# The retention gates as one half-size-products scheme over pairs of token tiles, with the steps reordered

## The chip, the cores and the metric

One NeuronCore of a Trainium2 chip. The metric is device time in microseconds of one execution. The whole model step is a single program with its instruction streams for TensorE (PE), VectorE (DVE), ScalarE (ACT), GpSimd (POOL) and SyncE (SP) written out by hand; the engines meet only at semaphores. All data are fp32.

## The reference

A two-layer diffusion trunk on 640 tokens: 512 latent and 128 prompt (context) tokens, five tiles of 128. Layer 0 mixes tokens by bidirectional retention with four heads, layer 1 by latent attention; each is followed by a mixture of experts. The change is in the retention layer:

```python
def step(s, xs):
    qc, kc, vc = xs
    att = einsum('bhnd,bhmd->bhnm', qc, kc) * intra
    o = einsum('bhnm,bhmv->bhnv', att, vc) + einsum('bhnd,bhdv->bhnv', qc * q_dec, s)
    s = s * c_dec + einsum('bhmd,bhmv->bhdv', kc * k_dec, vc)
    return s, o
...
q, k, v, g_f, g_b = split(h @ w_in)          # per head: q, k 256 wide, v, g_f, g_b 512 wide
o_f, s_f = retention_scan(q, k, v, ...)      # forward over chunks of 128 tokens
o_b, s_b = retention_scan(flip(q), ...)      # backward
y = silu(g_f) * head_layernorm(o_f, gn[0]) + silu(g_b) * head_layernorm(o_b, gn[1])
return y @ w_out, s_f, s_b
```

The prompt and the latent tokens are scanned apart: the prompt from a zero state, the latent tokens from a given one. The final prompt states are outputs.

## The kernel before

**Tiling.** `hT` holds the normalised input transposed, 8 slices of 128 features by 640 tokens (tiles 0 to 3 latent, tile 4, `PT`, prompt). Weights pass through five slots of 2 MB (`ring(0)` to `ring(4)`); slot 4 holds `XS`, sums of blocks of `hT`, in all heads. PSUM has eight banks of 128x512. The heads are head 0 (written out) and heads 1 to 3 (one loop body).

**A head.** First q and k (`products(h, 0, ...)`), then v (`products(h, 1, ...)`). Both already use the Strassen-Winograd scheme: for the 512 latent tokens, seven products of half-size blocks (`P1` to `P7`) in place of eight, with weight sums `T1` to `T4` made by DVE, a plain product `PR` for the prompt tile, and sums of the results by DVE (`u2`, `u3`, `C22`, `C21`, `C12`). In heads 1 to 3 the previous head's output projection (`out_proj`) stands between the two. Then the scores of five tiles (L1080), their masks by DVE (L1886, L1891), and ten steps.

**The steps.** `STEPS` lists the (tile, direction) pairs, latent ones first. In step i PE makes the output `o` in bank 5 (L1102; L1111 adds the part with the state, for latent tiles), updates the state where the step has one (L1119 into banks 6 and 7), transposes the next k (L1090), and makes the gate of this tile and direction: eight matmuls of 128x512 into one of banks 0 to 2 (L1127). Some steps also carry an eighth of the work on the modulation maps, a "slice" of `w_ada` (L891), and after four of them a panel transpose (L899). DVE: state update (L1912, or L1910 for the prompt), decayed k (L1897), statistics of `o` (L1919, L1921), normalisation (L1923, which frees bank 5), the gain (L1926), the gate (L1930, or L1932 and L1933 where the tile has its other direction already). POOL makes the reciprocal root (L776, L777) and the decayed q (L770). ACT applies silu to the gate bank (L1554).

**What sets the order.** Each engine's code, in order. PE's next step waits for L1923 of the last one, since there is one bank for `o`:

```python
if i:
    pe.wait_ge(S("o_free"), h * 10 + i)
```

**Borders.** After step 9 ACT writes the states out (L1564). In the next head it waits for `S_saved` (they have landed) and for the last step on DVE, issues three loads (L1542, L1544), and only then makes the copy `p1` (L1520) for which PE's `P2` of the q and k products waits:

```python
act.wait_ge(S("S_saved"), h * 32)
act.wait_ge(S("ln_done"), h * 10)
```

SP issues all weight loads through L524 in one written order, with a wait ahead of each for the last reader of its slot.

Of the kernel before, what the change touches and what calls it, by code (L numbers as in the profile page):

```python
# [39 lines left out]
STEPS = [(0, 0), (3, 1), (1, 0), (2, 1), (2, 0), (1, 1), (3, 0), (0, 1), (4, 0), (4, 1)]  # L40
STATE_STEPS = [0, 1, 2, 3, 4, 5, 8, 9]
NSS = len(STATE_STEPS)

SLICES_FIRST = {0: 0, 1: 1, 2: 2, 3: 3, 5: 4, 6: 5, 7: 6, 8: 7}
SLICES_LOOP = {1: 0, 3: 1, 5: 2, 7: 3}

SLOTS_FIRST = [0, 1, 0, 1, 0, 1, 0, 1]
SLOTS_LOOP = [0, 1, 0, 1]  # L50

PANELS_FIRST = {4: 1, 9: 2}
PANELS_LOOP = {8: None}
# [4 lines left out]


USES = 10  # L60
# [7 lines left out]

T_BANK = {0: (4, 6, 0, 2, 4), 2: (0, 0, 0, 0, 0)}
# [4 lines left out]
def use_base(h):  # L74

    return h * USES + PRE


def prod_no(h, f, name):

    return h * 16 + (f * 8 + PROD[name])


def add_no(h, f, name):

    return h * 18 + (4 + f * 9 + ADDS[name])


def copy_no(h, f, name):

    return h * 6 + (f * 3 + COPIES[name])
# [60 lines left out]
def build(nc, a, out):  # L152
    ctx = ExitStack()
    with ctx:
# [100 lines left out]
        sg = R["sg"].rearrange("p (b d) -> p b d", b=2)  # L255
        yy = R["y"].rearrange("p (t d) -> p t d", t=NT)
# [17 lines left out]
        def w_blocks(f, slot):  # L274
# [9 lines left out]
            return {"B11": b11, "B12": b12, "B21": b21, "B22": b22, "T1": b11, "T2": t2, "T3": b12, "T4": b21}  # L284

# [228 lines left out]
        def _(sp):  # L514
# [22 lines left out]
            for t in range(NT):  # L537
                src = a["x_prompt"][0] if t == PT else a["x_sample"][0, t * P:(t + 1) * P, :]
                sp.dma_start(x[:, t, :], src).then_inc(S(f"x_back{t}"), 16)

            def head_loads(h):
                first = isinstance(h, int)
                b = use_base(h)
                if not first:
                    sp.wait_ge(S("ada_done"), slices_done(h) - 1)
                for off in (0, RH * DK):
# [7 lines left out]
                for s, off in ((1, 2 * RH * DK), (2, 2 * RH * DK + RH * DV), (3, 2 * RH * DK + 2 * RH * DV)):  # L554
# [18 lines left out]
                else:  # L573
# [3 lines left out]
                    sp.wait_ge(S("op_done"), h * 10)  # L577
                    load_slice(1, h - 1, 1, SLOTS_LOOP[1])
                    sp.wait_ge(S("st_mm"), prod_no(h, 1, "P3"))
                    load_slice(1, h - 1, 0, SLOTS_LOOP[0])  # L580
                    for q in (2, 3):
                        sp.wait_ge(S("ada_done"), slices_done(h) + q - 1)
                        load_slice(1, h - 1, q, SLOTS_LOOP[q])
# [10 lines left out]
            sp.wait_ge(S("st_mm"), 16 * RH)  # L594
            load(4, ring(4).rearrange("p (j n) -> p j n", j=4), w_out[:, 12:16, :])

            def moe_loads(l):
# [6 lines left out]
                if l == 0:  # L604
                    sp.wait_ge(S("proj_done"), use_base(RH))
# [86 lines left out]
            for t in range(NT):  # L692
                sp.wait_ge(S("fin_ready"), t + 1)
                dst = out[0][0] if t == PT else out[1][0, t * P:(t + 1) * P, :]
# [7 lines left out]
        def _(pool):  # L702
# [55 lines left out]
            def head(h, per):  # L758
                def qdec_mul(u):
                    t, r = STEPS[u]  # L760
# [6 lines left out]
                    else:  # L767
                        pool.wait_ge(S("o_done"), h * 10 + u - 1)
# [5 lines left out]
                for i in range(10):  # L774
# [4 lines left out]
                    if i + 2 < 8:  # L779
                        qdec_mul(i + 2)  # L780
# [66 lines left out]
        def _(pe):  # L847
# [8 lines left out]
            def gate_bank_free(h, i):  # L856

                if i == 0:
                    pe.wait_ge(S("st_d"), add_no(h, 1, "C12"))
                elif i == 1:  # L860
                    pe.wait_ge(S("st_a"), copy_no(h, 1, "C11"))
                elif i >= 3:
                    pe.wait_ge(S("proj_evac"), use_base(h) + i - 2)

# [16 lines left out]
            def slice_of(h, panels_before, q, s):  # L881


                if q == 0:
                    pe.wait_ge(S("ada_act"), panels_before * 2)
                    pe.wait_ge(S("st_d"), add_no(h, 1, "C21"))
                pe.wait_ge(S(f"ring_full{s}"), full[s].next())
                for i in range(2):
                    k = 2 * q + i
                    for g in range(4):  # L890
                        mm = mmul(bank[3][32 * g:32 * g + 32, :], cond[:, 2 * k:2 * k + 32], ring2(s)[:, i, g * 512:g * 512 + 512],  # L891
# [74 lines left out]
            def out_proj(h, slot):  # L966
# [14 lines left out]
                for t in range(NT):  # L981
# [23 lines left out]
            def products(h, f, slot):  # L1005
# [17 lines left out]
                elif not first:  # L1023
                    pe.wait_ge(S("proj_evac"), use_base(h) - 2)
# [4 lines left out]
                elif not first:  # L1029
                    pe.wait_ge(S("ada_act"), h * 2 + 2)  # L1030
# [26 lines left out]

            def head(h):
# [3 lines left out]
                panels = PANELS_FIRST if first else PANELS_LOOP  # L1062
                b = use_base(h)
# [1234 lines left out]
```

## Time and profile before

| | us |
|---|---|
| median of 3 runs (lowest to highest) | 1860.96 (1854.48 to 1863.13) |
| the profiled execution's own time | 1861.93 |
| its span, first to last instruction | 1859.6 |
| PE busy | 1713.9 (92%) |
| DVE busy | 643.1 (35%) |
| mean granted TensorE clock, share of full | 0.964 |

An fp32 matmul stands in the trace as two PE instructions, so the eight matmuls of a gate are "x16". Matmul ends are modelled some 0.17 us late, so the start of one group to the start of the next is the better length. In a timeline, what stands in brackets is the idle time of the engine before the row and what ended it. Heads 0 to 3 end at about 240, 465, 685 and 905 us.

### The profile page before, as it was taken

What the parts mean: (1) busy time and instruction counts of PE and PEld (TensorE: products, weight loads), DVE (VectorE), ACT (ScalarE), POOL (GpSimd) and SP (SyncE); (2) the same over time, 40 slices, a digit from 0 to 9 for tenths busy, and PEclk for the clock granted to TensorE, in tenths of its full rate; (3) what the DMA queues carried; (4) which work ended last, traced back from release to release, by engine and by line L of the source; (5) the groups of instructions that cost most, each with busy time, mean ns of one, the idle gap of its engine ahead of it and who ended that gap; (6) DMA issues with size and microseconds to landing.
All of it is one profiled execution on the core that took longest, in us unless ns stands there. A gap on an engine that the chain in (4) does not pass through costs nothing.

```text
span 1859.6 us, 16869 instructions
## 1 busy us (share of the span) xinstructions
PE 1713.9 (92%) x6202; PEld 952.8 (51%) x6202; DVE 643.1 (35%) x1111; ACT 251.3 (14%) x538; POOL 180.8 (10%) x274
## 2 busy tenths in 40 slices
PE   4999999999999999999968999898999999689995
PEld 2864374644765456644444444354666664444442
DVE  2333323433233433333462332322333324423334
ACT  5000000000000000000121110321223221111111
POOL 1000000000001100010001222110000000012221
PEclk8999999999999999999987999999999999789998
DMA  9423452123412251112483999830000023749994
GB/s 339 160 91 136 147 212 90 46 91 136 147 45 90 74 183 70 67 68 90 148 293 125 342 341 349 251 119 0 23 22 5 7 81 124 238 128 342 345 344 139
DMA packets 159358, 281.21 MB, mean 151 GB/s; under 512 B 11428, under 2 KB 106424, under 8 KB 154184
## 3 DMA queue, kind: packets, MB, share of 16 engines
q1 hardware_dynamic: 144616, 236.39, 36.3%
q0 software_dynamic: 9248, 33.61, 6.9%
q10 hardware_dynamic: 5440, 10.49, 1.5%
q8 instruction: 34, 0.56, 0.1%
q14 instruction: 20, 0.16, 0.0%
HBM read 247.09 MB, written 33.37 MB: 151 GB/s over the span
## 4 chain that ended last, share of the span: by engine, by line
PE 78%; SPq 7%; DMA 7%; DVE 4%; issue 2%; ACT 1%; ACTq 0%; POOL 0%; DVEq 0%; POOLq 0%
PE banks L1127 15%; PE banks L1017 10%; PE banks L992 8%; PE banks L1189 7%; PE banks L1309 4%; PE banks L1408 4%; SPq L601 3%; PE banks L1206 3%; PE banks L1111 3%; PE banks L1119 3%; SPq L602 3%; PE banks L1102 2%; PE banks L891 2%; DMA wr<-in_moe_w_down 2%; PE banks L1341 2%
## 5 line engine op out<-in xcount | busy, mean ns | idle before, releaser
L1127 PE MATMUL banks<-wr 128*128 128x512 f32 x640 | 281.2, 592 | 0.0
L1189 PE MATMUL banks<-wr,arena 128*128 128x512 f32 x512 | 232.0, 607 | 9.8 <-DMA wr<-in_moe_w_down 6.5
L1127 PEld LDWEIGHTS banks<-wr 128*128 128x128 f32 x640 | 119.4, 190 | 139.7 <-issue 139.7
L1017 PE MATMUL banks<-wr 128*128 128x256 f32 x768 | 173.3, 385 | 4.1 <-ACT arena L1520 2.4
L1017 PEld LDWEIGHTS banks<-wr 128*128 128x128 f32 x768 | 147.8, 193 | 29.2 <-issue 4.5
L1189 PEld LDWEIGHTS banks<-wr,arena 128*128 128x128 f32 x512 | 96.9, 194 | 124.3 <-issue 123.5
L992 PE MATMUL banks<-wr,arena 128*128 128x512 f32 x320 | 142.9, 602 | 3.1 <-ACT arena L1514 3.1
L1206 PE MATMUL banks<-wr,arena 128*128 128x512 f32 x256 | 115.4, 593 | 0.9 <-ACT arena L1608 0.9
L992 PEld LDWEIGHTS banks<-wr,arena 128*128 128x128 f32 x320 | 60.4, 193 | 74.0 <-issue 72.0
L1554 ACT ACTIVATE arena<-banks 128x512 f32<-128x512 f32 x40 | 23.9, 597 | 520.4 <-PE banks L1127 520.4
L816 POOL DMA_INDIRECT acc_dram<-arena,put_ids x30 | 60.5, 2015 | 264.4 <-DVE arena L2065 264.4
L2050 DVE SCALAR_TENSOR_TENSOR arena<-banks,slot_w,arena 128x256 f32<-128x256 f32 x32 | 15.5, 484 | 183.2 <-ACT arena L1604 183.2
L1206 PEld LDWEIGHTS banks<-wr,arena 128*128 128x128 f32 x256 | 46.3, 190 | 48.3 <-issue 46.9
L1408 PE MATMUL banks<-wr,arena 128*128 128x512 f32 x160 | 70.3, 597 | 0.0
L2065 DVE TENSOR_TENSOR arena<-banks,arena 128x1024 f32<-128x1024 f32 x32 | 39.2, 1225 | 83.3 <-PE banks L1206 83.3
L1912 DVE SCALAR_TENSOR_TENSOR arena<-arena,cdec,banks 128x1024 f32<-128x1024 f32 x24 | 30.7, 1281 | 93.8 <-PE banks L1119 93.8
L1111 PE MATMUL banks<-arena 128*128 128x512 f32 x128 | 60.1, 592 | 0.0
L1119 PE MATMUL banks<-arena 128*128 128x512 f32 x128 | 60.1, 592 | 0.0
L770 POOL TENSOR_TENSOR arena<-arena 128x256 f32<-128x256 f32 x32 | 23.2, 730 | 376.5 <-DVE arena L1868 376.5
L1819 DVE TENSOR_TENSOR arena<-banks,arena 128x512 f32<-128x512 f32 x40 | 27.6, 691 | 84.6 <-PE banks L992 84.5
L1309 PE MATMUL banks<-arena 128*128 128x512 f32 (+1 forms) x192 | 54.0, 434 | 0.8 <-issue 0.8
L1359 PE MATMUL banks<-wr,arena 128*128 128x128 f32 x336 | 44.7, 277 | 8.0 <-DVE wr L2198 8.0
(269 smaller groups left out, 1968.1 us busy)
## 6 DMA issues: line engine op xcount, KB each, us to landing
wr<-in_w_ada SPq DMA_DIRECT2D x24, 2048.0 KB, 7.5
wr<-in_moe_w_gate SPq DMA_DIRECT2D x32, 1024.0 KB, 13.5
wr<-in_moe_w_up SPq DMA_DIRECT2D x32, 1024.0 KB, 16.2
wr<-in_moe_w_down SPq DMA_DIRECT2D x32, 1024.0 KB, 16.5
wr<-in_ret_w_in SPq DMA_DIRECT2D x12, 2048.0 KB, 10.7
wr<-in_ret_w_in SPq DMA_DIRECT2D x8, 1024.0 KB, 8.6
wr<-in_ret_w_out SPq DMA_DIRECT2D x4, 2048.0 KB, 7.6
arena<-mod_rows_dram SPq DMA_DIRECT2D x14, 512.0 KB, 6.8
```

What stands on the lines that cost most here:

```text
L601: sp.dma_start(gu[:, :, 1, :], w_u[l][e]).then_inc(S(f"w_full{b}"), 16)
L602: sp.dma_start(dn, w_d[l][e]).then_inc(S(f"w_full{b}"), 16)
L816: g.indirect_dma_start(out=acc[l], out_offset=bass.IndirectOffsetOnAxis(ap=put_ids[:, e:e + 1], axis=0), in_=ysb[:, b, :], in_offset=None, ...
L992: mm = mmul(bank[6 + hf][:], yT[:, t % 2, j, :], ring(slot)[:, j * D + hf * 512:j * D + hf * 512 + 512], start=(j == 0), stop=(j == 3))
L1017: mm = mmul(dst[:, r * 256:r * 256 + 256], lhs, rhs, start=(start and r == 0 and k == 0), stop=(k == 3), skip_group_check=True)
L1111: mm = mmul(bank[5][:], qd[:, i % 2, j, :], St[:, r, j, :], start=False, stop=(j == 1))
L1119: mm = mmul(bank[6 + j][:], kd[:, u % 2, tile_cols(j)], vv[:, t, :], start=True, stop=True)
L1127: mm = mmul(bank[i % 3][:], hT[:, k, tile_cols(t)], ring8(2 + r)[:, k, :], start=(k == 0), stop=(k == KT - 1))
L1189: mm = mmul(bank[2][:], xgT[:, e.par, k, :], expert_w(e.buf)[0][:, k].rearrange("p g f -> p (g f)"), start=(k == 0), stop=(k == KT - 1))
L1206: mm = mmul(bank[4 + 2 * e.par + hf][:], gactT[:, e.par, j, :], expert_w(e.buf)[1][:, j, hf * 512:hf * 512 + 512], start=(j == 0), stop=(j ...
L1309: mm = mmul(dst, lhs(k), rhs(k), start=(k == 0), stop=(k == nk - 1))
L1408: mm = mmul(bank[4 + hf][:], oTb[:, t % 2, k, :], w_o[:, k, hf * 512:hf * 512 + 512], start=(k == 0), stop=(k == KT - 1))
```

## The change

**Gates.** The ten gate products of a head are gone. The latent tiles are taken in pairs (0 and 1, the first half of the tokens; 2 and 3 the second), the forward and the backward gate weights (slots 2 and 3) as the two column blocks of one matrix, and the two halves of the features as its row blocks: the seven products of the scheme, each made for two tiles (`_0`, `_1`) with four matmuls of 128x512. The prompt tile keeps two plain products (`PR_0`, `PR_1`) of eight. That is 56 + 16 = 72 matmuls a head where there were 80. The weight sums are made in place by DVE, `T1`, `T2` ahead of step 0, `T3` after step 0, `T4` after step 1, each of 128x2048; ten result sums of 128x512 follow from step 1 on.

**Order.** `P1_0`, `P1_1`, `PR_0`, `PR_1` stand ahead of step 0, the others after steps 0 to 7, none after steps 8 and 9. The prompt's steps are first and have no state work there; step i (from 2) now does state i - 2. Tiles are held in the order 0, 1, 3, 2 (`ORDER`). In head 0 the first four slices go to bank 7 around steps 0 and 1.

```diff
-STEPS = [(0, 0), (3, 1), (1, 0), (2, 1), (2, 0), (1, 1), (3, 0), (0, 1), (4, 0), (4, 1)]
-STATE_STEPS = [0, 1, 2, 3, 4, 5, 8, 9]
-SLICES_LOOP = {1: 0, 3: 1, 5: 2, 7: 3}
+STEPS = [(4, 0), (4, 1), (0, 0), (2, 1), (1, 0), (3, 1), (3, 0), (1, 1), (2, 0), (0, 1)]
+STATES = [(0, 0), (2, 1), (1, 0), (3, 1), (3, 0), (1, 1), (4, 0), (4, 1)]
+SLICES_LOOP = {4: 0, 5: 1, 6: 2, 8: 3}
+SLICES_FIRST = {4: 4, 5: 5, 6: 6, 7: 7}
+SLOTS_LOOP = [1, 0, 1, 1]
+GBANK = {"P1_0": 1, "P2_0": 1, "P5_0": 1, "P3_0": 1, "P1_1": 0, "P2_1": 0, "P5_1": 0, "P3_1": 0, "PR_0": 3, "PR_1": 2,
+         "P6_0": 2, "P7_0": 2, "P6_1": 2, "P7_1": 2, "P4_1": 3, "P4_0": 3}
+AFTER_STEP = {0: ("P2_0", "P2_1"), 1: ("P6_0", "P7_0"), 2: ("P5_0", "P6_1"), 3: ("P7_1", "P5_1"), 4: ("P4_1",),
+              5: ("P3_1",), 6: ("P4_0",), 7: ("P3_0",)}
@@ SyncE, loads of a head
                     if s == 2 and not first:
-                        sp.wait_ge(S("proj_done"), b - 1)
+                        sp.wait_ge(S("st_mm"), gate_prod(h, "P4_0") - 32)
                     if s == 3 and not first:
-                        sp.wait_ge(S("proj_done"), b)
+                        sp.wait_ge(S("st_mm"), gate_prod(h, "P3_0") - 32)
@@ TensorE
+            def gate_product(h, name):
+                ...
+                elif p == "P7":
+                    pe.wait_ge(S("st_d"), gate_add(h, "u2_" + tile))
+                elif name == "P6_1":
+                    pe.wait_ge(S("st_d"), gate_add(h, "u3_0"))
+                ...
+                    cols = tile_cols(int(tile))
+                    for k in range(4):
+                        mm = mmul(dst, X[X_OF[p]][:, k, cols], W[p][:, k, :], start=(k == 0 and p not in ("P2", "P7", "P3")),
+                                  stop=(k == 3), skip_group_check=True)
+                mm.then_inc(S("st_mm"), 1)
                 ...
+                gate_product(h, "P1_0")
+                gate_product(h, "P1_1")
                 ...
+                pe.wait_ge(S("attm"), h * 4 + 4)
                 k_T(0)
+                gate_product(h, "PR_0")
+                gate_product(h, "PR_1")
                 ...
-                    for k in range(KT):
-                        mm = mmul(bank[i % 3][:], hT[:, k, tile_cols(t)], ring8(2 + r)[:, k, :],
-                                  start=(k == 0), stop=(k == KT - 1))
-                    mm.then_inc(S("proj_done"), 1)
+                    for name in AFTER_STEP.get(i, ()):
+                        gate_product(h, name)
@@ VectorE
+                sums = {1: ("u2_0", "T4", "u3_0"), 2: ("C22_0", "u2_1"), 3: ("u3_1", "C22_1"), 4: ("C21_1",), 5: ("C12_1",),
+                        6: ("C21_0",), 7: ("C12_0",)}
                 k_decay(0)
+                weight_sum("T1")
+                weight_sum("T2")
                 ...
+                    if i == 0:
+                        weight_sum("T3")
+                    for name in sums.get(i, ()):
+                        if name == "T4":
+                            weight_sum(name)
+                        else:
+                            gate_sum(name)
```

On DVE the statistics and the normalisation were behind the state update in a step; now the statistics are ahead of it. ACT copies `P1_0`, `P1_1`, and applies silu to four results in PSUM and to six in SBUF.

**The order of the instructions.** DVE in head 0, from the second weight sum to the sums after step 1. First what is there now (L1986 is `T2`, L1988 `T3`, L1992 `T4`, L2002 `u2_0` and `u3_0`, L2041 frees bank 5):

```order
L1986 TENSOR_TENSOR arena<-wr 128x2048 [waits st_d]
L2025 BN_STATS st<-banks 128x6 [waits o_done,gn_in,S_in]
L2027 BN_AGGR mv<-st 128x2 [waits dve_step]
L2041 TENSOR_SCALAR arena<-banks,mv,rv 128x512 [waits head_rstd]
L2044 TENSOR_TENSOR arena<-arena 128x512 [waits o_free]
L2049 TENSOR_TENSOR arena<-arena 128x512 [waits st_a,dve_step]
L1988 TENSOR_TENSOR wr<-wr 128x2048 [waits ln_done]
L2025 BN_STATS st<-banks 128x6 [waits o_done]
...
L2052 TENSOR_TENSOR arena<-arena 128x512 [waits dve_step]
L2002 TENSOR_TENSOR arena<-banks,arena 128x512 [waits st_a,st_mm,ln_done]
L1992 TENSOR_TENSOR wr<-arena,wr 128x2048 [waits st_mm,st_d]
L2002 TENSOR_TENSOR arena<-banks,arena 128x512 [waits st_a,st_mm]
```

Before, the first steps of DVE in head 0:

```order
L1897 TENSOR_SCALAR arena<-banks,kdec 128x256 [waits kt_done]
L1912 SCALAR_TENSOR_TENSOR arena<-arena,cdec,banks 128x1024 [waits S_done,gn_in,S_in]
L1897 TENSOR_SCALAR arena<-banks,kdec 128x256 [waits kt_done]
L1919 BN_STATS st<-banks 128x6 [waits o_done]
L1921 BN_AGGR mv<-st 128x2 [waits dve_step]
L1923 TENSOR_SCALAR arena<-banks,mv,rv 128x512 [waits head_rstd]
L1926 TENSOR_TENSOR arena<-arena 128x512 [waits o_free]
L1930 TENSOR_TENSOR arena<-arena 128x512 [waits proj_evac,dve_step]
```

Three weight sums and the whole of step 1 now stand ahead of the first `u2_0`; the state work has left these two steps.

PE in head 0, step 1 (L1170, `o`) with `P6_0`, `P7_0` and the panel transpose behind it, as it is now:

```order
L1170 MATMUL banks<-arena 128x512 [waits o_free]
L1116 MATMUL banks<-arena,wr 128x512 [waits st_d,st_a]
L1116 MATMUL banks<-arena,wr 128x512 x3
L1116 MATMUL banks<-wr 128x512 [waits st_d]
L1116 MATMUL banks<-wr 128x512 x3
L925 MATMUL banks<-ident,stage 128x128 [waits ada_act]
L925 MATMUL banks<-ident,stage 128x128 x3
```

Step 1 of PE before:

```order
L1102 MATMUL banks<-arena 128x512 [waits o_free]
L1111 MATMUL banks<-arena 128x512 [waits S_in,qd_ready]
L1111 MATMUL banks<-arena 128x512
L1119 MATMUL banks<-arena 128x512 [waits S_upd,kd_ready]
L1119 MATMUL banks<-arena 128x512
L1090 MATMUL banks<-ident,arena 128x128 [waits kd_ready]
L1090 MATMUL banks<-ident,arena 128x128
L1127 MATMUL banks<-wr 128x512 [waits ring_full3,st_a]
L1127 MATMUL banks<-wr 128x512 x7
```

The gate's eight matmuls waited for nothing that DVE makes within the steps; the second half of the eight that stand there now (`P7_0`, the second `st_d`) waits for a sum of the first.

SP keeps its order of loads. What changed is when the waits are met: slots 2 and 3 of the next head are free after steps 6 and 7, but their loads stand behind that of `w_out`, which waits for the last slice, now after step 8.

## Rows read from the trace of the kernel before

**Rows 1.** The page's first part: busy time of each engine.
```profile
PE 1713.9 (92%) x6202; PEld 952.8 (51%) x6202; DVE 643.1 (35%) x1111; ACT 251.3 (14%) x538; POOL 180.8 (10%) x274
```

**Rows 2.** Busy us of each engine in one 50 us stretch.
```profile
350.00:400.00 50.00, 50.00 (x146) 21.26 (x146) 19.11 (x29) 2.39 (x4) 5.74 (x12) 1.00 0.17 65
```

**Rows 3.** Waits (engine, line, releaser: us in total, times, longest).
```profile
PE banks L1090 <- DVE arena L1891: 5.8, 4, 1.5
...
PE banks L1017 <- ACT arena L1520: 2.4, 2, 1.4
```

**Rows 4.** Timeline of PE, one step of head 3 (start us, us, instructions).
```profile
801.50 1.02 PE L1102 MATMUL banks<-arena 128*128 128x512 f32 x2
...
804.08 1.88 PE L1119 MATMUL banks<-arena 128*128 128x512 f32 x4
805.80 0.38 PE L1090 MATMUL banks<-ident,arena 128*128 128x128 f32 x2
806.01 7.03 PE L1127 MATMUL banks<-wr 128*128 128x512 f32 x16
812.98 1.92 PE L891 MATMUL banks<-wr,cond 128*32 128x512 f32 x16
814.83 1.12 PE L1102 MATMUL banks<-arena 128*128 128x512 f32 x2
```

**Rows 5.** Timeline of DVE, steps 7 and 8 of head 3.
```profile
876.77 0.70 DVE L1919 BATCH_NORM_STATS2 st<-banks 128x6 f32<-128x512 f32 x1 [0.45 <-PE banks L1111]
...
878.74 0.81 DVE L1923 TENSOR_SCALAR arena<-banks,mv,rv 128x512 f32<-128x512 f32 x1 [0.93 <-POOL rv L777]
879.59 0.69 DVE L1926 TENSOR_TENSOR arena<-arena 128x512 f32<-128x512 f32 x1
...
888.34 1.23 DVE L1910 COPY arena<-banks 128x1024 f32<-128x1024 f32 x1 [2.57 <-PE banks L1119]
889.48 0.48 DVE L1897 TENSOR_SCALAR arena<-banks,kdec 128x256 f32<-128x256 f32 x1
889.88 0.69 DVE L1919 BATCH_NORM_STATS2 st<-banks 128x6 f32<-128x512 f32 x1
```

**Rows 6.** Timeline of DVE, two sums of 128x1024.
```profile
695.86 1.23 DVE L1850 TENSOR_TENSOR wr<-wr 128x1024 f32<-128x1024 f32 x1 [8.47 <-PE banks L1035]
697.12 1.23 DVE L1852 TENSOR_TENSOR arena<-wr 128x1024 f32<-128x1024 f32 x1
```

**Rows 7.** Timeline of PE after its longest waits near the heads.
```profile
242.20 0.28 PE L1138 MATMUL banks<-ident,mod 128*96 128x128 f32 x1 [2.34 <-DVE mod L1753]
242.52 5.40 PE L1017 MATMUL banks<-wr 128*128 128x256 f32 x16
...
907.42 1.18 PE L978 MATMUL banks<-ident,arena 128*128 128x128 f32 x8 [2.22 <-DVE arena L1933]
910.35 9.49 PE L992 MATMUL banks<-wr,arena 128*128 128x512 f32 x16 [1.75 <-ACT arena L1514]
```

**Rows 8.** Timeline of PE, the border between heads 2 and 3.
```profile
685.06 3.62 PE L1017 MATMUL banks<-wr 128*128 128x256 f32 x16
...
696.85 3.72 PE L1017 MATMUL banks<-wr 128*128 128x256 f32 x16 [1.02 <-ACT arena L1520]
```

**Rows 9.** Timeline of ACT, the same border.
```profile
685.49 0.96 ACTq L1564 DMA_DIRECT2D out<-arena  x2
694.59 0.41 ACTq L1542 DMA_DIRECT2D arena<-in_state_ret_fwd  x1
...
696.20 0.60 ACT L1520 ACTIVATE arena<-banks 128x512 f32<-128x512 f32 x1 [10.26 <-PE banks L1035]
```

**Rows 10.** ACT queue, DMAs issued at 46 us (KB each, us to landing).
```profile
arena<-in_state_ret_fwd ACTq DMA_DIRECT2D x1, 512.0 KB, 7.2
arena<-in_state_ret_bwd ACTq DMA_DIRECT2D x1, 512.0 KB, 9.5
```

**Rows 11.** DMAs issued on SP's queue from 33 to 44 us.
```profile
wr<-in_ret_w_in SPq DMA_DIRECT2D x3, 2048.0 KB, 20.2
```

More of the change, by code:

```diff
@@ L66 @@
 COPIES = {"p1": 1, "PR": 2, "C11": 3}
+GPROD = ("P1_0", "P1_1", "PR_0", "PR_1", "P2_0", "P2_1", "P6_0", "P7_0", "P5_0", "P6_1", "P7_1", "P5_1",
+         "P4_1", "P3_1", "P4_0", "P3_0")
+GADDS = ("T1", "T2", "T3", "u2_0", "T4", "u3_0", "C22_0", "u2_1", "u3_1", "C22_1", "C21_1", "C12_1", "C21_0", "C12_0")
+GCOPIES = ("p1_0", "p1_1", "PR_0", "PR_1", "C11_0", "C11_1", "C22_0", "C22_1", "C21_1", "C12_1", "C21_0", "C12_0")
+GBANK = {"P1_0": 1, "P2_0": 1, "P5_0": 1, "P3_0": 1, "P1_1": 0, "P2_1": 0, "P5_1": 0, "P3_1": 0, "PR_0": 3, "PR_1": 2,
+         "P6_0": 2, "P7_0": 2, "P6_1": 2, "P7_1": 2, "P4_1": 3, "P4_0": 3}
+AFTER_STEP = {0: ("P2_0", "P2_1"), 1: ("P6_0", "P7_0"), 2: ("P5_0", "P6_1"), 3: ("P7_1", "P5_1"), 4: ("P4_1",),
+              5: ("P3_1",), 6: ("P4_0",), 7: ("P3_0",)}
+GATE_OF = {(4, 0): "PR_0", (4, 1): "PR_1", (0, 0): "C11_0", (2, 1): "C22_0", (1, 0): "C11_1", (3, 1): "C22_1",
+           (3, 0): "C21_1", (1, 1): "C12_1", (2, 0): "C21_0", (0, 1): "C12_0"}
 T_BANK = {0: (4, 6, 0, 2, 4), 2: (0, 0, 0, 0, 0)}
@@ L255, in build @@
         sg = R["sg"].rearrange("p (b d) -> p b d", b=2)
+        late = R["yT"].rearrange("p (b d) -> p b d", b=2)
         yy = R["y"].rearrange("p (t d) -> p t d", t=NT)
@@ L1056, in products @@
                 product("P3", False)
+            def gate_product(h, name):
+                W = gate_w(isinstance(h, int))
+                p, tile = name.split("_")
+                if name == "P1_0":
+                    pe.wait_ge(S("ring_full2"), full[2].next())
+                    pe.wait_ge(S("st_a"), copy_no(h, 1, "C11"))
+                elif name == "P1_1":
+                    pe.wait_ge(S("st_d"), add_no(h, 1, "C12"))
+                elif name == "PR_1":
+                    pe.wait_ge(S("ring_full3"), full[3].next())
+                elif p == "P2":
+                    pe.wait_ge(S("st_a"), gate_copy(h, "p1_" + tile))
+                elif name == "P6_0":
+                    pe.wait_ge(S("st_a"), gate_copy(h, "PR_1"))
+                    pe.wait_ge(S("st_d"), gate_add(h, "T2"))
+                elif p == "P7":
+                    pe.wait_ge(S("st_d"), gate_add(h, "u2_" + tile))
+                elif name == "P6_1":
+                    pe.wait_ge(S("st_d"), gate_add(h, "u3_0"))
+                elif p == "P5":
+                    pe.wait_ge(S("st_a"), gate_copy(h, "C11_" + tile))
+                elif name == "P4_1":
+                    pe.wait_ge(S("st_a"), gate_copy(h, "PR_0"))
+                    pe.wait_ge(S("st_d"), gate_add(h, "T4"))
+                elif p == "P3":
+                    pe.wait_ge(S("st_d"), gate_add(h, "C22_" + tile))
+                elif name == "P4_0":
+                    pe.wait_ge(S("st_d"), gate_add(h, "C21_1"))
+                dst = bank[GBANK[name]]
+                if p == "PR":
+                    for k in range(KT):
+                        mm = mmul(dst, hT[:, k, TS:T], ring8(2 + int(tile))[:, k, :], start=(k == 0), stop=(k == KT - 1))
+                else:
[4 more added lines that the diff above has]
+                mm.then_inc(S("st_mm"), 1)
             def head(h):
```

250 lines of the change are left out of this document (147 added, 103 removed).

## The prediction

> **What bounds the kernel now.** I read the busy times first: PE is at 92% of the span, DVE at 35% [rows 1]. The averages hide stages, so next the windows: within the steps of a head PE is busy for all of 50 us at full clock, DVE for 19.1, ACT for 2.4 [rows 2]. The steps are bound by PE; a matmul taken out there is worth its length as long as DVE keeps up. Then the list of waits, for what PE stands still for in the heads: 1.45 us each for the masks (5.8 in four), and 1.0 and 1.4 at two borders between heads, for a copy by ACT [rows 3]. Last the timelines of PE and DVE, since the change turns independent products into a chain through DVE.
>
> **The unit prices.** A step of PE, by starts [rows 4]: `o` of a latent tile 2.58, the state 1.72, the k transposes 0.21, a gate of eight matmuls 6.97 with its hand-over, a slice 1.85. The gate and the slice together are 8.82, which I split as 6.9 and 1.9; four matmuls are 3.45, one 0.86. On DVE [rows 5]: statistics to normalisation 1.97 (POOL's root is in it), normalisation 0.85, each 128x512 operation after it about 0.72; a state update 1.14 to its follower, the decayed k 0.40. PE to DVE takes 0.2 to 0.3, DVE to PE about 0.1. A weight sum is 128x2048, a size the trace lacks. 128x1024 takes 1.23 [rows 6] and 128x512 takes 0.69 [rows 5]; the same slope gives 2.3 us. Bounds: 1.23 (as if size cost nothing) and 2.46 (twice). I take 2.3.
>
> **Removed, every head.** Eight matmuls net: -6.9. The mask wait: `P1_0` and `P1_1` now lie under it, -1.45 [rows 3].
>
> **Added, heads 1 to 3: the chain at `P7_0`.** Zero is the end of `PR_1` on PE. DVE can start `T1` at 0.2, so `T2` ends at 4.8. PE meanwhile makes `o` of step 0 (0.9) and `P2_0`, `P2_1` (7.7). DVE: statistics of step 0 at 4.8, normalisation 6.75 to 7.55, so bank 5 is free just as PE wants it; gain and gate to 9.0; `T3` to 11.3. PE: step 1 to 8.6, `P6_0` to 12.0. Only at 11.3 does DVE turn to step 1: 1.97 + 0.85 + three times 0.72 brings 16.3, `u2_0` 17.0. `P7_0` adds into the bank that `u2_0` reads, so PE stands from 12.0 to 17.0: **+5.0 us**. Behind it on PE's queue stand step 2 and all later ones. After this nothing in DVE's chain is late: `P6_1` finds `u3_0` done (step 2 lies between), `T4` is wanted only after step 4, and from step 4 on a step of PE is 2.58 + 1.72 + 0.21 + 3.45 = 8.0 or more, against 7.2 of DVE (1.98 to the state's end on PE, 1.14, 0.40, 0.85, three of 0.72, one sum of 0.7).
>
> **The end of the steps.** Bank 5 is free again 1.98 + 1.14 + 0.40 + 0.85 = 4.4 us after `o` ends. Step 8 has no gate product any more: 1.72 + 0.21 + slice 1.9 = 3.8 of work, so PE waits 0.6 before step 9. In head 0 step 8 has no slice either: 1.93 of work, 2.5 of wait. Net, without the clock: heads 1 to 3 -6.9 - 1.45 + 5.0 + 0.6 = **-2.8 each**.
>
> **The clock.** PE ran at full clock after waits of 1.0 and 1.4 (16 half-size instructions in 3.72 [rows 8]), but after a wait of 2.34 the same 16 took 5.40, and after 2.22 and 1.75 close together 16 of 128x512 took 9.49 where 7.0 is usual [rows 4, 7]: 1.8 and 2.5 us lost at half clock, 1.2 in place of 2.4 GHz. A wait of 5.0 is longer than all of these. I charge 1.8, bounds 0 and 2.5, to each new wait above 2.2: heads 1 to 3 come to -1.0 each, **-3.0**.
>
> **Head 0.** Two slices lie in the first part and give DVE time on PE's side: step 1's `o` ends at 12.5, `P6_0` at 16.0, `u2_0` at 18.4, a wait of 2.4. With 2.5 before step 9 and 1.8 of clock for both: -6.9 - 1.4 + 2.4 + 2.5 + 3.6 = +0.2. At its end PE's transpose of the modulation rows waits for DVE (2.34 now [rows 7]). DVE's last step was under a gate product; now it starts with PE's last matmuls and ends 1.98 + 1.14 + 0.85 + three of 0.72 = 6.1 after `o`, 4.0 after PE's last work at 2.15, and three small operations follow: 4.7 in place of 2.3, **+2.4**.
>
> **The borders before heads 2 and 3.** PE stops at 685.06, wants `p1` at 685.06 + 10.8, and gets it 1.0 late [rows 8]. ACT had issued the states at 685.49, their landing let it go on at 694.59, 1.6 us of issues and a copy of 0.6 follow [rows 9]. Now the last state is updated 3.1 us after step 9's `o`, so the issue comes 1.1 after PE's end, not 0.43: +0.7. And more is in flight: `w_out` and slots 2 and 3, 6 MB, are released together about 5 us before PE's end, where one load of 2 MB was. What does that do to 1 MB on ACT's queue? At 46 us two loads of that size landed in 7.2 and 9.5 us [rows 10] while SP's queue held 2 MB loads that took 20.2 each [rows 11]: ACT's queue is not made to wait for SP's. So 9.1 becomes 9.5 to 10: +0.2 to +0.8. Waits of about 2.2 and 2.6, **+1.2 each**, and in half of them the clock falls, +0.9 each: +4.2 for both. Before head 1 PE arrives later than ACT and nothing changes. After head 3 the projection's transposes wait 4.0 for DVE, not 2.2, and its first matmuls come at 6.2 after PE's end, not 5.3: +0.9 [rows 7].
>
> The Trainium skill ("DMA: Bandwidth & Descriptors", Queues, rings and completion order) says two things that pull apart: each DMA engine takes turns between its queues packet by packet, which would give the states their half; but a completion semaphore is a strongly ordered write that lands only after all earlier writes of that engine, also those of other queues. Rows 10 and 11 bear out the first; by the second alone the borders would come out as in the second rival.
>
> **The sum.** -3.0 + 0.2 + 2.4 + 4.2 + 0.9 = **+4.7** on the profiled execution's 1861.9 (span 1859.6): 1866.6. It is 1.0 above the median of the runs, so I predict 1865.5. The case's own bounds: no clock lost at all and +0.6 a border gives -8.4 - 3.4 + 2.4 + 1.2 + 0.9 = -7.3 (1853.5 as a median); 2.5 of clock at every wait and +1.5 a border gives +12.0 (1873).
>
> **The rivals.**
> *The gain is paid out.* If DVE's chain never reached PE, only the removed work would count: 4 x 6.9 + 5.8 = -33, some 1828. For it: DVE is at 35%. Against: the timeline has PE and DVE in lock-step through one bank, and the average says nothing of steps 0 and 1, where DVE has 17 us of work for PE's 12. 5%.
> *The weight sums are cheap.* At 1.23 each (the lower bound) `u2_0` comes 3.2 us earlier, the wait is 1.8 and the clock stays up: 3 x (3.2 + 1.8) = 15 less, 1850.5. The two rows of different size speak against it. 8%.
> *The states wait for all weights* (the slow side). If a landing is told only when all that was issued before has drained, then from the 9.1 us that 3 MB (1 MB of states, 2 MB of slot 3) take at this border now [rows 9], the 5.7 MB left then take some 17: PE waits 9 at the two borders instead of 1.0 and 1.4, +9.8 each with the clock, +19.6 in place of +4.2: 1881. It decides as soon as the landing takes over 11. Rows 10 and 11 are against it. 12%.
> *The change doesn't save what it says:* the program counts 72 for 80, so no.
>
> **Chances.** The forecast 75%, its own range 1853.5 to 1873; above 1870.3 lies a tenth of the whole. A measurement of this kernel can't tell less than 0.5% (9.3 us) from no change. Faster by more: 5 + 8 and a little of the forecast's low end, 16%. Slower by more: 12 + 10, 22%. The rest, 62%, within. Range 1851 to 1875.
>
> **What would show it.** After: PE L1116 waiting about 5 us, three times, for DVE L2002, once 2.4 in head 0, with a slow window behind; L1170 waiting 0.6 in heads 1 to 3 and 2.5 in head 0 for L2041; PE L1153 waiting for no mask; DVE at 128x2048 2.3 us; the `p1` copy's wait at two borders 2 to 3 us; L1206 waiting 4.7. PE's matmul count falls by 64 instructions. I am wrong in the size if the wait for L2002 is below 3 us, or if full clock follows it; wrong in kind if the heads get shorter by over 5 us, or if PE waits for a DMA (a slice) in a step.

## The result and the profile after

The changed kernel takes 1867.41 us (median of 9 runs) where the kernel before took 1861.54 beside it: ratio 1.0031 [1.0019, 1.0044]. It is slower by about 6 us, which is within 0.5%. One of the nine runs took 2084.41 at a granted clock of 0.826, and the ratio leaves it out. The profiled execution took 1864.86 (span 1862.5, mean granted clock 0.960), against 1861.93, 1859.6 and 0.964.

The page's first part, to be held against [rows 1]: 20 us less of PE, 63 more of DVE.

```profile
PE 1693.8 (91%) x6138; PEld 944.5 (51%) x6138; DVE 706.0 (38%) x1167; ACT 257.4 (14%) x546; POOL 180.8 (10%) x274
```

So PE does 20 us less and the span is 2.9 longer: 23 us went into standing still. The list of PE's waits in the four heads (us in total, times, longest) says where; it answers to [rows 3].

```profile
PE banks L1116 <- DVE arena L2002: 17.4, 4, 5.0
PE banks L1043 <- ACT arena L1588: 6.6, 2, 3.5
PE banks L1206 <- DVE mod L1832: 4.3, 1, 4.3
PE banks L1004 <- DVE arena L2052: 3.9, 1, 3.9
PE banks L1170 <- DVE arena L2041: 3.3, 4, 2.2
PE banks L1043 <- DVE arena L1931: 2.7, 1, 2.7
```

The mask waits are gone. In their place stand the chain at `P7_0` (first row), the borders before heads 2 and 3 (second), the ends of heads 0 and 3 (third, fourth), bank 5 before step 9 (fifth), and one that the prediction didn't have: `P6` of head 1's q and k, which waits for a weight sum (sixth).

Head 1's steps 0 to 2 on PE (start, duration, group, in brackets the idle time before it):

```profile
370.12 1.02 PE L1170 MATMUL banks<-arena 128*128 128x512 f32 x2
370.98 7.03 PE L1116 MATMUL banks<-wr 128*128 128x512 f32 x16
377.85 1.02 PE L1170 MATMUL banks<-arena 128*128 128x512 f32 x2
378.71 3.60 PE L1116 MATMUL banks<-wr 128*128 128x512 f32 x8
387.33 6.46 PE L1116 MATMUL banks<-wr 128*128 128x512 f32 x8 [5.03 <-DVE arena L2002]
```

DVE in the same 17 us, from `T1` (L1983) to `u2_0` (the last row):

```profile
370.32 2.29 DVE L1983 TENSOR_TENSOR wr<-wr 128x2048 f32<-128x2048 f32 x1 [13.14 <-PE banks L1112]
372.65 2.29 DVE L1986 TENSOR_TENSOR wr<-wr 128x2048 f32<-128x2048 f32 x1
374.86 0.69 DVE L2025 BATCH_NORM_STATS2 st<-banks 128x6 f32<-128x512 f32 x1
...
379.21 2.29 DVE L1988 TENSOR_TENSOR wr<-wr 128x2048 f32<-128x2048 f32 x1
381.42 0.69 DVE L2025 BATCH_NORM_STATS2 st<-banks 128x6 f32<-128x512 f32 x1
...
385.77 0.69 DVE L2052 TENSOR_TENSOR arena<-arena 128x512 f32<-128x512 f32 x1
386.58 0.69 DVE L2002 TENSOR_TENSOR arena<-banks,arena 128x512 f32<-128x512 f32 x1
```

From 370.32 on DVE stands still only for POOL's root (0.94 us each time) and for 0.16 us behind each of the statistics. `o` of step 1 ends on PE at about 378.8, but `T3` holds DVE until 381.4, and the whole of step 1's normalisation stands ahead of `u2_0`. PE waits 5.03 us for a sum of 0.69. The window answers to [rows 2]: PE busy 44.97 us where it was 50, DVE 21.12, and the granted clock 0.93 where it was 1.00 (busy us of PE, PEld, DVE, ACT, POOL, then the clock).

```profile
350.00:400.00 50.00, 44.97 (x102) 19.68 (x101) 21.12 (x26) 3.58 (x6) 2.92 (x7) 0.93 0.00 0
```

The border before head 2, PE and then ACT. At the next one, that of [rows 8] and [rows 9], the wait was 3.08 and the landing took 10.6.

```profile
466.04 3.62 PE L1043 MATMUL banks<-wr 128*128 128x256 f32 x16
469.49 7.31 PE L1059 MATMUL banks<-wr 128*128 128x128 f32 x64
480.29 5.41 PE L1043 MATMUL banks<-wr 128*128 128x256 f32 x16 [3.49 <-ACT arena L1588]
```

```profile
467.06 0.94 ACTq L1643 DMA_DIRECT2D out<-arena  x2
478.05 0.41 ACTq L1618 DMA_DIRECT2D arena<-in_state_ret_fwd  x1
...
479.64 0.60 ACT L1588 ACTIVATE arena<-banks 128x512 f32<-128x512 f32 x1 [13.08 <-issue]
```

The states go out 1.0 us after PE's last work, as forecast, and ACT goes on 11.0 us later. "Landing" below is this stretch, from the first of ACT's two issues to its next one; the view of the DMAs counts each transfer from its own issue and gives a median, so it says 9.2 for the same two. What lay in the queues at that time (KB each, us to landing):

```profile
wr<-in_ret_w_in SPq DMA_DIRECT2D x2, 2048.0 KB, 18.5
wr<-in_ret_w_out SPq DMA_DIRECT2D x1, 2048.0 KB, 7.7
out<-arena ACTq DMA_DIRECT2D x2, 512.0 KB, 9.2
```

**Where the time went.** The starts of the same group in both profiled executions, and the difference:

| group | before | after | difference |
|---|---|---|---|
| scores of head 0 | 112.07 | 112.06 | 0 |
| first q/k product of head 1 | 242.52 | 242.79 | +0.3 |
| scores of head 1 | 345.59 | 347.07 | +1.5 |
| first q/k product of head 2 | 464.72 | 466.04 | +1.3 |
| products past that border (64 instructions behind `P6`) | 483.89 | 488.98 | +5.1 |
| first q/k product of head 3 | 685.06 | 688.93 | +3.9 |
| products past that border | 703.86 | 711.47 | +7.6 |
| first transposes of the experts | 988.17 | 994.87 | +6.7 |
| end of the span | 1859.6 | 1862.5 | +2.9 |

The last row but one is where the retention layer's account closes; it is close to the medians (+5.9). What comes after it is unchanged code, and took between 864.8 and 873.4 us in the twelve traces.

### The profile page after: what moved, and what is told of

Same layout as the page of the kernel before. It is cut to its first block, busy times and chain, and to the rows that moved or that the text cites. A ratio compares the mean times of both kernels' runs of the same rounds, so it can differ in the third digit from the quotient of the medians.

```text
span 1862.5 us, 16824 instructions
## 1 busy us (share of the span) xinstructions
PE 1693.8 (91%) x6138; PEld 944.5 (51%) x6138; DVE 706.0 (38%) x1167; ACT 257.4 (14%) x546; POOL 180.8 (10%) x274
## 4 chain that ended last, share of the span: by engine, by line
PE 70%; DMA 8%; issue 8%; SPq 7%; DVE 5%; ACT 1%; POOL 1%; ACTq 0%; POOLq 0%; DVEq 0%
PE banks L1043 10%; PE banks L1116 8%; PE banks L1257 7%; PE banks L1018 7%; PE banks L1377 4%; PE banks L1476 4%; SPq L640 3%; PE banks L1274 3%; PE banks L1178 3%; PE banks L1187 3%; SPq L641 3%; DMA wr<-in_moe_w_down 2%; PE banks L1408 2%; PE banks L1409 2%; PE banks L1340 2%
## 5 line engine op out<-in xcount | busy, mean ns | idle before, releaser
L1116 PE MATMUL banks<-wr 128*128 128x512 f32 x432 | 198.2, 608 | 17.4 <-DVE arena L2002 17.4
L1043 PEld LDWEIGHTS banks<-wr 128*128 128x128 f32 x768 | 149.9, 196 | 33.5 <-ACT arena L1588 6.9
L1116 PEld LDWEIGHTS banks<-wr 128*128 128x128 f32 x432 | 81.8, 196 | 113.2 <-issue 92.5
L1898 DVE TENSOR_TENSOR arena<-banks,arena 128x512 f32<-128x512 f32 x40 | 27.6, 691 | 81.5 <-PE banks L1018 81.2
L2025 DVE BATCH_NORM_STATS2 st<-banks 128x6 f32<-128x512 f32 x40 | 27.9, 698 | 73.9 <-PE banks L1178 72.3
L1112 PE MATMUL banks<-wr 128*128 128x512 f32 x128 | 55.7, 593 | 0.0
L1607 ACT ACTIVATE arena<-arena 128x512 f32<-128x512 f32 x24 | 15.1, 629 | 280.1 <-DVE arena L2005 134.6
```

The costliest lines, as they stand in the source:

```text
L1043: mm = mmul(dst[:, r * 256:r * 256 + 256], lhs, rhs, start=(start and r == 0 and k == 0), stop=(k == 3), skip_group_check=True)
L1116: mm = mmul(dst, X[X_OF[p]][:, k, cols], W[p][:, k, :], start=(k == 0 and p not in ("P2", "P7", "P3")), stop=(k == 3), skip_group_check=True)
```

## The experiments

The theory: the product's gain goes to four waits, of which the chain at `P7_0` is the largest and the borders the second. The rival for the chain is that DVE simply has too much work there, so that its order doesn't matter; for the borders, that the slow landing has nothing to do with the weight loads. The kernel before took 1861.98 to 1862.75 beside these runs; each ratio is to it, with its 95% interval in brackets.

**e1: the first sum ahead of step 1's normalisation.**

```diff
                     v.bn_aggr(mv[:, i % 2, :], st6[:]).then_inc(S("stats"), 1)
+                    if i == 1:
+                        gate_sum("u2_0")
                     if i >= 2:
...
-                sums = {1: ("u2_0", "T4", "u3_0"), ...
+                sums = {1: ("T4", "u3_0"), ...
```

> The changed kernel with one edit: DVE makes u2_0 between the statistics and the normalisation of step 1, not after the whole of step 1. Theory (PE's wait at P7_0 is DVE's order, and the half clock behind it is the wait's doing): P6_0 ends at 382.2 in the changed kernel's trace and DVE's statistics of step 1 at 382.45, so u2_0 ends at 383.15 and P7_0 starts 4.1 us earlier in each of heads 1 to 3; the wait left is about 1.0, the clock stays full there, which gives back 2.9, 1.8 and 1.5 more; head 0 wins 1.4. Sum -20: some 1847.5 us. Rival (the 5 us only move: DVE is short of time in steps 2 and 3, so PE waits there instead): within 5 us of 1867. Rival (the half clock is not caused by the wait): about -13.5, 1854.

Measured: 1850.83, ratio 0.9931 [0.9913, 0.9949]. DVE does the same work in the same time. PE at `P7_0` of head 1:

```profile
377.14 3.60 PE L1116 MATMUL banks<-wr 128*128 128x512 f32 x8
381.61 3.70 PE L1116 MATMUL banks<-wr 128*128 128x512 f32 x8 [0.87 <-DVE arena L2002]
```

0.87 in place of 5.03, and full clock behind it: 3.70 us where there were 6.46. That is 16.6 us less than the changed kernel for one moved line, where 20 were expected: half clock now came at head 1's `P6` (5.41 behind a wait of 2.99) and lasted longer at the border before head 2 (6.77 for 5.41). The chain was a matter of order; the rival falls.

**e7: the weight sums made tiny.** The four weight sums cover 128x1 elements and `P6` takes a plain block of the weights; the sums of the weights are left out of the computation.

```diff
-                        ins = v.tensor_tensor(g_b11, g_b12, g_b11, ALU.subtract)
+                        ins = v.tensor_tensor(t2[:, 0, 0:1], g_b12[:, 0, 0:1], g_b11[:, 0, 0:1], ALU.subtract)
...
```

> The changed kernel with the four weight sums of 128x2048 cut to 128x1 and the sixth product taken from a plain weight block, so the gates are not the reference's: it prices the weight sums apart from DVE's order. Theory: without T1 and T2 DVE is free for step 0 at once, and u2_0 waits only for the rest of step 1: PE's wait at P7_0 is 8.6 + 0.2 + 1.97 + 0.85 + 4 x 0.72 = 14.5 less 12.0 = 2.5 us, not 5.0, so half of that wait is order and half the sums. The step before 9 is unchanged. Some 2.5 x 3 less, and up to 2 of half clock in each: 1855 to 1860. Rival (the sums are all of the wait): below 1 us left.

Measured: 1853.73, ratio 0.9959 [0.9942, 0.9976]. PE at `P7_0` of head 1:

```profile
384.25 5.40 PE L1116 MATMUL banks<-wr 128*128 128x512 f32 x8 [2.52 <-DVE wr L1992]
```

The tiny `T4` stands right behind `u2_0` on DVE and bears the name here; heads 2 and 3 wait the same 2.52 and name `u2_0`'s line. Even with nothing to do for the weight sums, half of the wait stays, and more time stays than with the order of e1 (1853.73 against 1850.83, with wide spreads). So of the 5.0 half belongs to the weight sums (one, `T3`, takes 2.29) and half to step 1's own work, which e1 puts behind the sum.

**e3 and e10: a slice after step 8 of head 0.** The fourth slice moves from step 7 to step 8, to cover the wait of 2.21 before step 9. Both are the same kernel; it was run again, since the profiled run of e3 stood still for 2.6 and 5.6 us at the border before head 2, which no row explains.

```diff
-SLICES_FIRST = {4: 4, 5: 5, 6: 6, 7: 7}
+SLICES_FIRST = {4: 4, 5: 5, 6: 6, 8: 7}
```

> The changed kernel with one number changed: in head 0 the last slice stands after step 8, not 7, as in heads 1 to 3. Theory: the wait before step 9 in head 0 falls from 2.2 to 0.35 us and the half clock in step 9 (1.7 us lost) goes: -3.5, some 1864. Rival (the clock falls anyway, being about to fall at the border): -1.9. Either is at the edge of what the times can tell; the trace of head 0 decides.

> The changed kernel with head 0's last slice after step 8, again, for a trace: the first one had a pause of 7 us at the border before head 2 that no engine explains. Theory: PE's wait before step 9 of head 0 is 0.35 us, step 9 runs at full clock, head 1 begins about 3.5 us earlier than in the changed kernel, counted from the scores of head 0. Rival (the clock falls there anyway): 1.9 earlier.

Measured: 1865.71, ratio 1.0017 [1.0008, 1.0026], and again 1869.85, ratio 1.0026 [1.0007, 1.0044]. The first lies 1.7 below the changed kernel and the second 2.4 above, where 1.9 to 3.5 less was expected; only the trace can tell what the slice does. The pause didn't come back. The wait before step 9 is 0.35 and head 0 is shorter: from its scores to the modulation-row transpose 126.7 us in both runs (111.87 to 238.54 in e10) for 130.4. Yet head 2 begins at 465.60, only 0.4 earlier than after the change. PE of e10 in head 1:

```profile
238.54 0.28 PE L1206 MATMUL banks<-ident,mod 128*96 128x128 f32 x1 [4.34 <-DVE mod L1832]
238.87 5.35 PE L1043 MATMUL banks<-wr 128*128 128x256 f32 x16
...
259.58 5.24 PE L1043 MATMUL banks<-wr,arena 128*128 128x256 f32 x16 [4.77 <-DVE arena L1931]
```

and the same two places of the changed kernel:

```profile
242.79 5.36 PE L1043 MATMUL banks<-wr 128*128 128x256 f32 x16
...
261.46 3.72 PE L1043 MATMUL banks<-wr,arena 128*128 128x256 f32 x16 [2.71 <-DVE arena L1931]
```

Head 0 ends 3.9 us earlier. `P6` starts 1.9 earlier and, at half clock, ends 0.4 earlier. DVE of e10 names what holds it:

```profile
257.04 1.23 DVE L1929 TENSOR_TENSOR wr<-wr 128x1024 f32<-128x1024 f32 x1 [18.65 <-DMA arena<-mod_rows_dram]
```

Head 1's first weight sum stands on DVE behind the wait for the gate rows of the modulation, which go out from SBUF and come back on POOL's queue. Their round trip sets where `P6` starts; a shorter head 0 only makes PE wait longer there. The same place in the changed kernel:

```profile
246.72 0.41 ACTq L1618 DMA_DIRECT2D arena<-in_state_ret_fwd  x1
247.58 1.82 POOL L824 DMA_DIRECT2D arena<-mod_rows_dram  x2 [3.39 <-DMA mod_rows_dram<-mod_rows]
258.92 1.23 DVE L1929 TENSOR_TENSOR wr<-wr 128x1024 f32<-128x1024 f32 x1 [16.59 <-PE banks L1043]
```

and in the kernel before:

```profile
248.78 1.82 POOL L785 DMA_DIRECT2D arena<-mod_rows_dram  x2 [4.86 <-DMA mod_rows_dram<-mod_rows]
250.52 0.41 ACTq L1542 DMA_DIRECT2D arena<-in_state_ret_fwd  x1
257.45 1.22 DVE L1850 TENSOR_TENSOR wr<-wr 128x1024 f32<-128x1024 f32 x1 [15.39 <-DMA arena<-mod_rows_dram]
```

The row of the changed kernel names PE, but the product for which this sum waits (`PR`) ended at 255.3; the rows landed just ahead of 258.92. The weights were not beside them there: their last load, issued at 225.95, had landed 18.6 us later, at 244.5. (In e10 the last one did lie beside them, until 256.2.) What moved is ACT's three loads of 512 KB, issued from 0.9 us ahead of the rows on, where they were 1.7 behind. That they are the cause is not shown, since no run moves them alone. The border the prediction left out ("before head 1 nothing changes") has an owner of its own.

**e2: the loads held until the states have landed.** SP waits ahead of `w_out` for the states of the last head, so all 6 MB go out later.

```diff
                     sp.wait_ge(S("ada_done"), slices_done(h))
+                    sp.wait_ge(S("S_saved"), h * 32)
                     load(1, ring(1)
```

> The changed kernel with one edit: SP issues w_out and the loads of slots 2 and 3 for the next head only once the states have landed. Theory (the states land late because 6 MB of weights are in flight on the other queue): the landing falls from 11.0 and 10.6 us after the issue to about 4.5, as after head 3, PE's waits of 3.5 and 3.1 us for the copy go, and the half clock behind them (1.7 each): -10 us, some 1857.5. Rival (the landing is late because the states are written late, and costs what it costs): less than 2 us gained. Head 1 is left as it is by both, or worse by up to 2, since the weights then run beside the modulation rows.

Measured: 1863.84, ratio 1.0011 [0.9996, 1.0025]. At the border before head 2 the states land in 4.4 us and PE doesn't wait. But in head 1:

```profile
255.46 3.62 PE L1044 MATMUL banks<-wr 128*128 128x256 f32 x16
266.85 5.57 PE L1044 MATMUL banks<-wr,arena 128*128 128x256 f32 x16 [7.78 <-DVE arena L1932]
```

The 6 MB now fall on the gate rows, which take 11.8 us to land, 9.9 after the change and 6.4 before it. I had expected 10 us from the borders and at most 2 lost here, and the kernel gained 3.6 in all. So loads do slow what lies in another queue beside them, POOL's too.

**e6: held until the states and the gate rows are there.** As e2, with one wait more: `sp.wait_ge(S("g1_in0"), 32)`.

> The changed kernel with the last of these edits alone. Theory (head 1's 7.8 us wait in the run before was the modulation rows beside 6 MB of weights): with the weights behind both, the P6 wait of head 1 is at most 1.5 us, the borders before heads 2 and 3 stay without a wait: 1867.4 - 10 - 1.2 = 1856. Rival (head 1 waits because its weights or gain come later): the 7.8 us stay, 1864.

Measured: 1855.12, ratio 0.9975 [0.9962, 0.9987], as expected. The borders' waits and that of head 1 are gone, those at `P7_0` stay (5.03, 5.01, 5.02). The borders and the entry of head 1 cost the changed kernel 12 us together, and holding the loads takes that away. At the borders this is direct. At head 1 it is not, since no weights lay beside the rows in the changed kernel: here the states are told sooner (4.5 us for 7.7), ACT's loads go out 4.4 us ahead of the rows, and the rows take 6.7.

**e8: the kernel before, with its loads late.** Only the weight loads of the kernel before are bunched as the change bunches them: `w_out` also waits for the last gate product, so that 6 MB are issued just ahead of the states.

```diff
                     sp.wait_ge(S("ada_done"), slices_done(h))
+                    sp.wait_ge(S("proj_done"), b)
                     load(1, ring(1)
```

> The kernel before with one wait more on SP: w_out and slots 2 and 3 of the next head are all issued after the last gate product, 6 MB ahead of the states, which are issued as they were. Theory (weights in flight slow the states' landing by sharing, but do not hold it to their own end): the landing goes from 9.1 to 9.5 us to about 11, PE's waits of 1.0 and 1.4 us to about 3 each, head 1 waits 2 to 3 us for its sums: +5 to +8 us on the kernel before, some 1868. Rival (it is told only when all 7 MB have drained, 18 us or more): waits of 8 us and over, +20.

Measured: 1875.42, ratio 1.0082 [1.0063, 1.0102]. ACT and PE at the border before head 2:

```profile
470.46 1.02 ACTq L1565 DMA_DIRECT2D out<-arena  x2
482.18 0.41 ACTq L1543 DMA_DIRECT2D arena<-in_state_ret_fwd  x1
```

```profile
484.41 3.72 PE L1018 MATMUL banks<-wr 128*128 128x256 f32 x16 [3.62 <-ACT arena L1521]
```

The landing takes 11.7 us there and 11.55 at the next border, the waits are 3.62 and 3.44, and `P6` of head 1 waits 4.08 where it waited 1.46. No product was touched: the timing of the loads alone makes such borders. The waits at the borders came as expected, that in head 1 was 1 us above, and the time 7 us above: 4.7 of wait at the borders, 2.6 in head 1 and two stretches of 5.4 at half clock (3.4) are 10.7 of the 13.4 us lost; the rest isn't settled.

**e4: the mask wait of the kernel before covered.** Two of the eight matmuls of gate 0 stand ahead of the wait for the masks.

```diff
+                gate_bank_free(h, 0)
+                pe.wait_ge(S("ring_full2"), full[2].next())
+                gate_part(0, range(2))
                 pe.wait_ge(S("attm"), h * 4 + 4)
```

> The kernel before with one edit: two of the eight matmuls of step 0's gate stand ahead of PE's wait for the masks, the other six where they were. Theory (the masks' wait is worth its 1.45 us a head, and the change got that part in full): -5.8 on the kernel before, some 1855.7. Rival (PE then waits as long before step 1, since bank 5 comes free 6.3 us after step 0's o and only 7.1 us of work lie there): no gain.

Measured: 1858.69, ratio 0.9981 [0.9971, 0.9992], 3.7 less than before, where 5.8 were expected. The mask waits are gone and a head takes 218.5 and 218.1 for 220.35 and 219.97. Part of what the change gains needs no half-size product.

**e5: all three repairs in the changed kernel.** e1, e3 and the hold of e6.

> The changed kernel with three edits: u2_0 early on DVE, head 0's last slice after step 8, and w_out and slots 2 and 3 of the next head issued only when the states have landed and, for head 1, the gate rows of the modulation too. Theory (the lost time is these waits): u2_0 early took 16.5 us off, the borders before heads 2 and 3 cost 3.4 + 3.4 of wait and some 1.7 + 1.7 of half clock, and head 1's 2.7 us wait for its weight sums returns to the 1.5 of the kernel before; the slice is worth up to 3. Sum from 1850.8: -10 - 1.2 - 2 = 1837.5, faster than both kernels. Rival (the weights, issued later, come late for the output projection): PE would wait there, over 1845.

Measured: **1828.97**, ratio 0.9825 [0.9812, 0.9838], the fastest of all. PE's waits in the heads:

```profile
PE banks L1208 <- DVE mod L1834: 4.3, 1, 4.3
PE banks L1006 <- DVE arena L2056: 3.9, 1, 3.9
PE banks L1118 <- DVE arena L2004: 3.4, 4, 0.9
...
PE banks L1172 <- DVE arena L2045: 1.4, 4, 0.4
```

and the border before head 2, which has no wait:

```profile
452.65 3.62 PE L1045 MATMUL banks<-wr 128*128 128x256 f32 x16
456.11 7.31 PE L1061 MATMUL banks<-wr 128*128 128x128 f32 x64
463.25 2.11 PE L1045 MATMUL banks<-wr 128*128 128x256 f32 x9
```

Scores to scores a head takes 211.6 us, against 220.2 before (mean) and 224.0 and 222.5 after the change. e1 and e6 alone gave 16.6 and 12.3; e5 gives 38.4, 9.5 more. The slice, worth nothing alone, counts here, since `P6` of head 1 follows without a wait: it starts 142.1 us after the scores of head 0, for 146.5 in e6, 4.4 earlier, of which 1.6 are the shorter wait at `P7_0`. That is about 2.8 for the slice. For most of the other 6.7 the traces say where it lies. From the scores of head 0 to the first transposes of the experts e1 gains 17.4, e6 10.5 and e5 36.4, 8.5 more than both: 3.0 of it ahead of head 1's scores, 1.9 in heads 1 and 2, and 3.5 from head 3's scores on. There the first 16 matmuls of the last projection, partly at half clock, took 10.14 us in e1 and 10.20 in e6, but 8.82 in e5 and 7.88 after the change. So e1 and e6 alone each lost some of their gain again to half clock, and e5 did not; why it lasts longer in one run than in another isn't shown.

**e9: the kernel before with its own two repairs.** e4's edit, and slot 3's load held for states and gate rows, to see what e5 owes to the products.

```diff
-                        sp.wait_ge(S("proj_done"), b)
+                        sp.wait_ge(S("S_saved"), h * 32)
+                        sp.wait_ge(S("g1_in0"), 32)
```

> The kernel before with two edits: two matmuls of step 0's gate ahead of the masks' wait, and the load of slot 3 for the next head issued when the states have landed (and, for head 1, the gate rows), not after the last gate product. It prices the small repairs without the half-size products. Theory (the borders' waits of 1.35 and 0.94 us, and head 1's 0.66 and 1.49, are the 2 MB in flight beside the states): they go, 1858.7 - 4 = 1855, so that 25 us of the best kernel's gain (1829.0) are the products' own. Rival (the loads held back were worth more than PE's waits show, as the best kernel came out 8.5 below its sum): 1848 or less.

Measured: 1853.22, ratio 0.9949 [0.9931, 0.9967]. The borders' waits are gone, that at head 1's `P6` stays (1.56). So 9.5 us are in reach without the half-size products, and 24 us lie between the two repaired kernels, near the 4 x 6.9 = 27.6 that the removed matmuls take. The two differ in the order of the steps too, so the 24 us are not shown to be the products' alone.

## Why the prediction was right

1865.5 was predicted with a range of 1851 to 1875 and 62% for no measurable change; 1867.41 and +0.31% came. Step by step:

- **Removed work: right.** 64 matmul instructions fewer, PE 20.1 us less busy (27.6 less of full-speed matmuls, given back in part at half clock), no mask wait.
- **The chain at `P7_0`: right.** +5.0 forecast, 5.03, 5.01 and 5.01 measured; 2.4 and 2.35 in head 0. 2.3 for a sum of 128x2048, 2.29 measured. e7 gives the terms apart.
- **Heads 1 to 3: right, with the clock.** -3.0 forecast; -0.2, -1.2 and -1.5 measured, -2.9. Without the clock it is -3.0 in each, for the -2.8 of the sum. The loss of clock was charged at 1.8 each; the eight instructions behind the wait took 6.46, 5.40 and 5.11 in place of 3.60, which is 2.9, 1.8 and 1.5. Bank 5 before step 9: 0.35 for the 0.6 forecast.
- **Head 0: 2.3 us too high.** The steps were to come out at +0.2 and came out at -1.7; its end at +2.4, and the wait went from 2.34 to 4.33, +2.0. The failed term is the clock: 1.8 charged for both waits, but behind the wait of 2.35 the eight instructions of `P7_0` took 3.70, full speed (in e2 they took 5.25 behind the same wait, so here luck decides). Behind the 2.21 before step 9 half speed came (3.53 for 1.88), as charged.
- **The borders before heads 2 and 3: 3.3 too low.** +4.2 forecast, +3.8 and +3.7 measured. The step that failed was "9.1 becomes 9.5 to 10": the landing took 11.0 and 10.6 at the two borders, where it had been 9.5 and 9.1: +1.5 each time. The states lose to 6 MB in SP's queue more than the loads of [rows 10] did beside [rows 11]. The waits were 3.5 and 3.1, not 2.6 and 2.2, and half clock followed both times, where I had counted one time in two. e8 shows this cost in the kernel before, e6 takes it away.
- **The entry of head 1: missed.** "Before head 1 PE arrives later than ACT and nothing changes" is true of ACT and says nothing of DVE. The weight sum behind the gate rows was late by 2.71, not 1.46: +1.2. The rows landed in 9.9 us for 6.4. Beside them lay no weights (these had landed by 244.5) but ACT's own loads for the next head, which now go out ahead of the rows, and which the prediction did not look at. In e6, where the states and the rows run apart from the weights and ACT's loads are earlier still, the rows take 6.7 and PE does not wait.
- **After head 3: right.** +0.9 forecast, +0.6 by the two timelines; waits of 3.87 for 4.0.

The misses partly cancel: -2.3 in head 0, +3.3 at the borders, +1.2 at the entry of head 1. The agreement within 2 us is in part luck; the sign and the mechanism of the loops are not.

**The rivals.** *The gain is paid out* (1828): false for this kernel. That the three repairs bring it to 1829 is in part chance, since they also take away the borders' waits, which that sum left standing. *The weight sums are cheap* (1850.5): false, 2.29 each. *The states wait for all weights* (1881; the prediction calls it the second rival, and it stands third): false. The Trainium skill ("DMA: Bandwidth & Descriptors", Queues, rings and completion order) has both rules; by the strongly ordered write alone, as the prediction read it, the states would have come with the loads. They were told landed 11.0 us after their issue, at 478.05, while the two loads of slots 2 and 3 took 18.5 (median); the last of them, issued at 462.26, took 21.3 and landed at 483.5. That fits the turns by packet, with a price that the prediction put too low: at 11.0 the landing was just at the point from which that rival was to decide.

## What to carry to other kernels

When PE is at 92% and DVE at 35%, half-size products still have to be priced by the first chain of DVE that PE meets: put the sum that PE waits for ahead of all that it doesn't wait for, in DVE's order. And when a change frees several buffers at once, list every transfer in flight beside the loads it releases, on every queue, and hold the loads until all the short transfers on which an engine waits have landed (held for the states alone, in e2, they fell on the gate rows). A wait covered ahead of another wait (e10) gained nothing that the runs could show while the second stood.

## What the runs showed that I had not expected

- **The length of a wait doesn't tell whether the clock falls.** Full speed followed waits of 3.62 (e8, above), 3.52 (e7), 2.71 and 2.35; half speed (1.2 in place of 2.4 GHz) followed 3.49, 3.08, 2.52 and 2.21. The same wait in the same place has both: behind 2.35 in head 0 eight instructions took 3.70 after the change and 5.25 in e2, behind 2.21 four took 3.53 after the change and 1.88 in e1. e7 has both in one run: 5.40 behind 2.52 within the steps, and at the border before head 2

```profile
465.35 7.31 PE L1059 MATMUL banks<-wr 128*128 128x128 f32 x64
476.17 3.72 PE L1043 MATMUL banks<-wr 128*128 128x256 f32 x16 [3.52 <-ACT arena L1588]
```

  Behind every wait of more than 4 us in the heads it fell: 5.41 for 16 half-size instructions behind 4.08 (e8), 5.36 behind 4.33, and 6.46, 5.40, 5.11 for eight behind 5.0 (6.19 in e6). A charge of half the loss for each wait of 2 to 4 us would have been the better guess.
- **A short transfer beside long ones.** The 1 MB of states on ACT's queue landed in 4.4 us with no weights beside it (e2), 9.1 and 9.5 with one load of 2 MB issued just ahead (before), and 10.6 to 11.7 with 6 MB (after, e8).
